# Second block's sparse attention: values padded as the stationary side, weights transposed by reciprocal row sums one feature chunk further on

## The reference, cut to what matters

```python
def sparse_attention(q, k, v, q_idx, k_idx, w_idx, rel_bias):
    ...
        score = jnp.where(s_pos[None, None, :] <= t_pos[None, :, None], score, -jnp.inf)
        _, idx = lax.top_k(score, topk)
    ...
        logits = jnp.where(valid[:, :, None, :], logits, -jnp.inf)
        p = jax.nn.softmax(logits, axis=-1).astype(v.dtype)
        o = jnp.einsum('bqhk,bqkhd->bqhd', p, vs)
        return o.reshape(B, Q_BLOCK, BRANCH_W)
```

## Time and profile before

| | us |
|---|---|
| median of 3 runs | 1947.67 |
| lowest and highest | 1947.66, 1947.9 |
| the profiled execution | 1947.58 |
| its span in the trace | 1945.9 |
| PE busy in it | 1926.0 (99%) |
| DVE busy | 1379.2 (71%) |
| ACT busy | 926.0 (48%) |
| POOL busy | 238.2 (12%) |

### The profile page before, as it was taken

The page is one execution under the profiler, slowest core; times in us unless marked ns, Lnnn a source line. Parts: engine busy times, 40 slices in busy tenths (PEclk is TensorE's granted clock), DMA queues, the critical chain, the costliest instruction groups (busy, mean ns, idle before and its releaser), DMA issues.

```text
span 1945.9 us, 29897 instructions
## 1 busy us (share of the span) xinstructions
PE 1926.0 (99%) x11936; PEld 1721.2 (88%) x11936; DVE 1379.2 (71%) x1577; ACT 926.0 (48%) x1020; POOL 238.2 (12%) x196
## 2 busy tenths in 40 slices
PE   7999999999999999999999999999999999999998
PEld 6999888889998888888899998888888899998887
DVE  7686766677677666766769677667766769677666
ACT  5564433445644443644554445444544554445443
POOL 0000000000001000000049250000000049250000
PEclk9999999999999999999999999999999999999999
DMA  7544555554355555555454455555555454555553
GB/s 269 195 159 152 188 184 192 195 192 173 132 195 205 194 192 175 186 191 181 167 183 152 171 190 191 185 194 175 205 192 181 167 183 152 173 190 180 185 192 108
DMA packets 50483, 353.37 MB, mean 182 GB/s; under 512 B 5921, under 2 KB 6049, under 8 KB 8657
## 3 DMA queue, kind: packets, MB, share of 16 engines
q1 hardware_dynamic: 47952, 341.93, 49.6%
q0 software_dynamic: 2432, 10.04, 1.6%
HBM read 349.85 MB, written 2.10 MB: 181 GB/s over the span
## 4 chain that ended last, share of the span: by engine, by line
PE 89%; DVE 6%; ACT 2%; issue 1%; DMA 0%; DVEq 0%; SPq 0%; POOL 0%; POOLq 0%; ACTq 0%
PE ps L225 19%; PE ps L189 18%; PE ps L191 18%; PE ps L190 18%; PE ps L226 9%; DVE w_lo L165 3%; PE ps L229 3%; PE ps L228 1%; ACT w_hi L158 1%; DVE conv_y L2021 1%; PE ps L1184 1%; DVE score L2069 0%; ACT a L1565 0%; PE ps L2202 0%; DVE top L2064 0%
## 5 line engine op out<-in xcount | busy, mean ns | idle before, releaser
L165 DVE TENSOR_TENSOR w_lo<-raw,w_hi 128x2048 fp32r<-128x2048 f32 x318 | 736.5, 2319 | 283.4 <-ACT w_hi L158 282.3
L158 ACT ACTIVATE w_hi<-raw 128x2048 fp32r<-128x2048 f32 x318 | 608.0, 1916 | 402.3 <-PE ps L191 225.7
L225 PE MATMUL ps<-a,w_hi 128*128 128x512 f32 x1568 | 563.2, 398 | 2.3 <-DVE w_lo L165 1.3
L226 PE MATMUL ps<-a,w_lo 128*128 128x256 f32 x1568 | 439.9, 281 | 0.0
L225 PEld LDWEIGHTS ps<-a,w_hi 128*128 128x128 f32 x1568 | 295.0, 188 | 67.5 <-DVE w_lo L165 2.4
L189 PE MATMUL ps<-mixH,w_hi 128*128 128x256 f32 x1168 | 334.4, 286 | 0.6 <-DVE w_lo L165 0.4
L190 PE MATMUL ps<-mixL,w_hi 128*128 128x256 f32 x1168 | 330.4, 283 | 0.0
L191 PE MATMUL ps<-mixH,w_lo 128*128 128x256 f32 x1168 | 330.3, 283 | 0.0
L189 PE MATMUL ps<-w_hi,mixH 128*128 128x512 f32 x832 | 324.9, 390 | 1.0 <-DVE mixL L397 0.9
L191 PE MATMUL ps<-w_hi,mixL 128*128 128x512 f32 x832 | 323.8, 389 | 0.0
L190 PE MATMUL ps<-w_lo,mixH 128*128 128x512 f32 x832 | 323.7, 389 | 0.0
(11 more groups left out here) (378 smaller groups left out, 2274.8 us busy)
## 6 DMA issues: line engine op xcount, KB each, us to landing
raw<-in_w_b SPq DMA_DIRECT2D x198, 1024.0 KB, 5.0
raw<-in_w_a SPq DMA_DIRECT2D x125, 1024.0 KB, 4.8
rows<-in_post_gains POOLq DMA_DIRECT2D x6, 512.0 KB, 4.1
rows<-in_rows_a POOLq DMA_DIRECT2D x2, 1028.0 KB, 7.1
raw<-in_w_a SPq DMA_DIRECT2D x2, 512.0 KB, 5.9
x<-in_x SPq DMA_DIRECT2D x2, 512.0 KB, 5.9
bias_line<-a_gates POOLq DMA_DIRECT2D x1, 1024.0 KB, 4.2
out<-x SPq DMA_DIRECT2D x4, 256.0 KB, 2.0
```

The source lines that it names most:

```text
L158: act.activation(k.w_hi[:, s, :], k.raw[:, s, :], ACT.Copy).then_inc(k.hi_ready, 1)
L165: dve.tensor_tensor(k.w_lo[:, s, :], k.raw[:, s, :], k.w_hi[:, s, :].bitcast(F32), ALU.subtract).then_inc(k.lo_ready, 1)
L225: pe.matmul(both, hi[:, kt, cols], k.a[:, :, kt, :], start=kt == 0, stop=False)
L226: pe.matmul(high, lo[:, kt, cols], k.a[:, 0, kt, :], start=False, stop=False)
```

## The change

The values `v_tok` are stored padded: each head has 128 columns, of which its own 64 hold values and the other 64 zeros, so that two heads of a pair can be summed into one tile of 128 features. They become the stationary side, the weights `pT` the moving side, and the result comes out by feature in PSUM bank 3, where the transposes of `yb2` put it before; `yb2`, its transposes and VectorE's reciprocals and products go. The division by the row sums moves in front: ScalarE's exponentials write their row sums, GpSimd raises them to the power -1 and multiplies the identity by them (`rdiag`, in the place of `qkF`), and the 12 transposes of the weights become 12 matmuls by these diagonals. These stand behind feature 17 instead of in front of it, the weighted sums stand behind feature 18, and on ScalarE `gate_in(8)` moves in front of the evictions of `pT`. GpSimd's order gets the new work between its last tap and the wait for VectorE's taps.

```diff
-        v_tok = sb("b_v_tok", [P, TT, BH, BD + 1])
+        v_tok = sb("b_v_tok", [P, TT, BH, 2 * BD])
+        v_own = v_tok[:, :, :, :].rearrange("p t (j e) d -> p t j e d", e=2)
+        rdiag = qkF[:, :, :].rearrange("p f n -> p (f n)").rearrange("p (t h n) -> p t h n", t=TT, h=BH)
+        neg_one = sb("neg_one", [P, TT, BH])
...
-        yb2 = sb("yb2", [P, TT, BW])
         gated = [[RL[:, n * 512:(n + 1) * 512] for n in range(3)] + [y0[:, :, :].rearrange("p t n -> p (t n)")],
-                 [GU[:, n * 512:(n + 1) * 512] for n in range(3)] + [yb2[:, :, :].rearrange("p t n -> p (t n)")]]
+                 [GU[:, n * 512:(n + 1) * 512] for n in range(3)] + [idxF[:, :, :].rearrange("p f n -> p (f n)")]]
...
+            pool.memset(neg_one[:, :, :], -1.0).then_inc(zc.sem, zc.one())
+            pool.wait_ge(zc.sem, zc.at(0))
+            pool.memset(v_tok[:, :, :, :], 0.0).then_inc(vzero_ready.sem, 1)
...
                 pool.wait_ge(ch.sem, ch.at(l))
+                pool.wait_ge(exp_ready.sem, exp_ready.at(l, 2))
+                pool.tensor_tensor(rsum[:, :, :], rsum[:, :, :], neg_one[:, :, :], ALU.pow).then_inc(ch.sem, ch.one())
+                pool.wait_ge(ch.sem, ch.at(l))
+                for qt in range(TT):
+                    ins = pool.tensor_tensor(rdiag[:, qt], mid(k.ident, BH), last(rsum[:, qt, :], P), ALU.mult)
+                ins.then_inc(rdiag_ready.sem, 1)
...
+                if l == 0:
+                    act.wait_ge(vzero_ready.sem, vzero_ready.at(0, 1))
                 act.wait_ge(k.chunk_done, st.results(l, M0 + 2))
                 for tt in range(TT):
-                    ins = act.activation(v_tok[:, tt, :, 0:BD], k.ps[:, 0, tt * BW:(tt + 1) * BW].rearrange("p (h n) -> p h n", h=BH),
-                                         ACT.Copy, scale=rho[:, tt:tt + 1])
+                    v = k.ps[:, 0, tt * BW:(tt + 1) * BW].rearrange("p (j e n) -> p j e n", j=2, e=2)
+                    for e in range(2):
+                        ins = act.activation(v_own[:, tt, :, e, e * BD:(e + 1) * BD], v[:, :, e, :], ACT.Copy, scale=rho[:, tt:tt + 1])
                 ins.then_inc(f_evicted.sem, 1)
...
-                                             bias=rmax[:, qt, h:h + 1])
+                                             bias=rmax[:, qt, h:h + 1], accum_out=rsum[:, qt, h:h + 1])
...
                 gate_in(7)
+                gate_in(8)
                 act.wait_ge(pT_done.sem, pT_done.at(l, 1))
...
-                gate_in(8)
...
-            dve.memset(v_tok[:, :, :, BD:BD + 1], 1.0).then_inc(vone_ready.sem, 1)
...
-                dve.wait_ge(pv_done.sem, pv_done.at(l, 1))
-                y2v = yb2[:, :, :].rearrange("p t (j e n) -> p t j e n", j=2, e=2)
-                outs = [k.ps[:, (5, 2)[qt], 0:BH * (BD + 1)].rearrange("p (e j n) -> p e j n", e=2, j=2) for qt in range(TT)]
-                for qt in range(TT):
-                    dve.reciprocal(rsum[:, qt, :].rearrange("p (e j) -> p e j", e=2), outs[qt][:, :, :, BD]).then_inc(ch.sem, ch.one())
-                dve.wait_ge(ch.sem, ch.at(l))
-                for qt in range(TT):
-                    for e in range(2):
-                        ins = dve.tensor_tensor(y2v[:, qt, :, e, :], outs[qt][:, e, :, 0:BD],
-                                                last(rsum[:, qt, 2 * e:2 * e + 2], BD), ALU.mult)
-                ins.then_inc(y2_ready.sem, 1)
...
+                feature(17)
                 pe.wait_ge(exp_ready.sem, exp_ready.at(l, 2))
+                pe.wait_ge(rdiag_ready.sem, rdiag_ready.at(l, 1))
                 for h in range(BH):
                     for kb in range(2):
-                        ins = pe.transpose(k.ps[:, 2 + h // 2, (h % 2) * SEQ + kb * P:(h % 2) * SEQ + (kb + 1) * P], logit[:, h, (1 + kb) * P:(2 + kb) * P], k.ident)
+                        ins = pe.matmul(k.ps[:, 2 + h // 2, (h % 2) * SEQ + kb * P:(h % 2) * SEQ + (kb + 1) * P],
+                                        logit[:, h, (1 + kb) * P:(2 + kb) * P], rdiag[:, 1, h, :], start=True, stop=True)
                 ins.then_inc(pT_done.sem, 1)
                 for h in range(BH):
-                    ins = pe.transpose(k.ps[:, 4, h * P:(h + 1) * P], logit[:, h, 0:P], k.ident)
+                    ins = pe.matmul(k.ps[:, 4, h * P:(h + 1) * P], logit[:, h, 0:P], rdiag[:, 0, h, :], start=True, stop=True)
                 ins.then_inc(pT_done.sem, 1)
-                feature(17)
+                feature(18)
                 pe.wait_ge(pT_ready.sem, pT_ready.at(l, 2))
-                for qt in range(TT):
-                    for h in range(BH):
-                        j, e = head_slot(h)
-                        out = k.ps[:, (5, 2)[qt], (2 * e + j) * (BD + 1):(2 * e + j + 1) * (BD + 1)]
-                        for s in range(qt + 1):
-                            ins = pe.matmul(out, pT[:, 2 * e + j, s + qt, :], v_tok[:, s, h, :], start=s == 0, stop=s == qt)
-                ins.then_inc(pv_done.sem, 1)
-                feature(18)
-                pe.wait_ge(y2_ready.sem, y2_ready.at(l, 1))
-                to_features(3, yb2).then_inc(y2T_done.sem, 1)
+                for j in range(BH // 2):
+                    out = k.ps[:, 3, j * SEQ:(j + 1) * SEQ]
+                    pe.matmul(out, v_tok[:, 0, 2 * j, :], pT[:, j, 0:2, :], start=True, stop=False)
+                    for e in range(2):
+                        pe.matmul(out[:, P:SEQ], v_tok[:, 1, 2 * j + e, :], pT[:, 2 * e + j, 2, :], start=False, stop=False)
+                    ins = pe.matmul(out, v_tok[:, 0, 2 * j + 1, :], pT[:, 2 + j, 0:2, :], start=False, stop=True)
+                ins.then_inc(y2T_done.sem, 1)
```

More of the change, by code:

```diff
@@ L50 @@
 DVE_A = 112
-CARRIED = {n: n for n in ("sc_done", "pT_done", "pT_ready", "pv_done", "max_ready", "exp_ready", "mix_ready", "mixH_ready",
+CARRIED = {n: n for n in ("sc_done", "pT_done", "pT_ready", "max_ready", "exp_ready", "mix_ready", "mixH_ready",
                           "mix_split", "f_evicted")}
@@ L1250 @@
 TAKEN = float(np.float32(-3.3e38))
-DVE_B = 109
-POOL_B = 63
+DVE_B = 107
+POOL_B = 64
 def second_block(nc, k, d, sems, block):
@@ L1365, in second_block @@
         sc_done, l_ready, max_ready, exp_ready = sig("sc_done", 2), sig("l_ready", 2), sig("max_ready", 2), sig("exp_ready", 2)
-        pT_done, pT_ready, pv_done, y2_ready, y2T_done, y2H_ready, y2_split = (
-            sig(n, p) for n, p in (("pT_done", 2), ("pT_ready", 2), ("pv_done", 1), ("y2_ready", 1), ("y2T_done", 1),
+        pT_done, pT_ready, rdiag_ready, y2T_done, y2H_ready, y2_split = (
+            sig(n, p) for n, p in (("pT_done", 2), ("pT_ready", 2), ("rdiag_ready", 1), ("y2T_done", 1),
                                    ("y2H_ready", 1), ("y2_split", 1)))
-        vone_ready = sig("vone_ready", 0)
+        vzero_ready = sig("vzero_ready", 0)
         pmm_done, y1H_ready, y1_split = (sig(n, 1) for n in ("pmm_done", "y1H_ready", "y1_split"))
```

## The result

| | before | after |
|---|---|---|
| median, us (19 runs each) | 1947.62 | 1951.09 |
| lowest to highest | 1947.22 to 1947.93 | 1950.89 to 1952.02 |
| the profiled execution | 1947.58 | 1951.01 |
| its span | 1945.9 | 1949.3 |

The ratio is 1.0018, 95% interval 1.0013 to 1.0024: the changed kernel is 3.47 us slower. The slowdown is clear of noise. At 0.18% it lies just under the 0.2% by which the prediction sorts slower from unchanged, and its interval reaches over that line on the upper side. It is within the stated range of 1950.9 to 1957.3, 0.5 under the forecast of 1951.6.

A forecast was written before the change was run, and what follows sets the result against it. TensorE, busy 99% of the span, was taken to bound the kernel. Layers +1.65 and +2.06 make 3.71, plus 2 x 0.1 gives 3.9: 1951.5 profiled, median 1951.6; range 1950.9 to 1957.3.

The forecast's parts named there:

- Order: On TensorE, chunk 17 directly after chunk 16 still waits for w_lo until 1071.88; 1.6 us idle a layer, transposes move behind.
- The sum from chunk 17 to chunk 20: TensorE, start to start: 23.00 us against 21.35 in layer 0 (+1.65) and 20.94 in layer 1 (+2.06).
- rdiag matmuls: On TensorE behind chunk 17, 12 one-pass transposes become 12 matmuls by a diagonal, 24 passes, 2.60 us.
- padded sums with the chunk behind them: On TensorE behind chunk 18, 8 two-pass matmuls taking 2.53 us, then chunk 19 at 5.83.
- The wait before chunk 20: TensorE's 0.52 us wait for w_lo in layer 0 goes, since all of TensorE is later.
- GpSimd's power: Power of 8 columns after GpSimd's 16 taps: 0.56 plus 7 x 0.14, estimated 1.6 us.
- the power's hold on VectorE: Delay of VectorE while GpSimd's power runs: between 0 and 1.6 us, taken as 0.1 a layer.
- The products: GpSimd's two 512-column products, 1.36 us each, fall on taps after w_lo(17), delaying w_lo(18) by 2.1, covered by 1.0.
- Rival C: GpSimd's power holds the port, so products get ahead of w_lo(17): 2.4 to 3.5 a layer, 1956.2 to 1958.4; chance 0.20.
- Rival B: GpSimd's products slip in first, holding w_lo(17) or making w_lo(18) miss chunk 18: 1.05 a layer, 1953.6; chance 0.15.
- D: Not slower: w_lo(17) arrives during chunk 16, chunk 17 follows at once, 1.6 less a layer, 1948.4; chance 0.05.
- E: The matmuls by the diagonal take one pass like transposes, 1.3 less a layer, 1949.0; chance 0.03.

The follow-up runs named there:

- e1: Changed kernel with VectorE computing w_lo of chunk 17 right behind that of chunk 16, the four taps between them afterwards; 1947.82 us, ratio to before 1.0002.
- e2b: Kernel before with the new order alone, old matmuls, no new GpSimd work, w_lo(21) also ahead of VectorE's wait for the result by feature; 1949.56 us, ratio 1.0011.
- e3: New matmuls in the old order, multiplying by the identity, without GpSimd's power and products; 1947.74 us, ratio to before 1.0002.
- e6: Kernel before with only VectorE's order changed: w_lo(17) right behind w_lo(16), w_lo(20) before the wait for the evicted result; 1946.23 us, ratio 0.9993.
- e5: Changed kernel with GpSimd's power of the row sums replaced by a multiplication of the same tiles; 1957.11 us (1955.33 to 1958.66 in five runs).

## Why the prediction was right, step by step

- *Order*, the deciding step: right. Chunk 17 starts some 1.6 later than an ordinary step and waits for `w_lo`(17), and e1 and e2b show it from both sides: with the wait taken out of the changed kernel, 3.0 to 3.3 come back; with the order put into the kernel before, 2.0 are lost.
- *The sum from chunk 17 to chunk 20*: 23.00 forecast, 23.02 and 23.03 measured. Its terms: rdiag matmuls 2.60 forecast, 2.60 measured (1077.55 to 1080.15); padded sums with the chunk behind them 2.53 + 5.83 = 8.36 forecast, 8.38 measured (1085.98 to 1094.36). Order alone costs 2.0 (e2b), the matmuls alone 0.35 (e3), both 3.5. The traces say why these don't add up. From the end of chunk 16 to chunk 20, e1 (new matmuls) takes 23.02 and e6 (old matmuls) 22.04 in each layer, with hardly a wait in either. So the new matmuls are 1.0 more work a layer, 2.0 in all. The waits beyond that were 0.91 and 0.53 before and are 1.58 and 1.60 in the changed kernel, 1.7 more. The change thus costs about as much by added work as by added waiting: in the old order the old waits pay for most of that work, in the new order nothing does.
- *The wait before chunk 20* is gone, as said.
- *GpSimd's power*: 1.6 forecast from the rise of 0.14 a column, 1.74 measured, and 1.75 in layer 1. The forecast passed over the one row of two columns that took 1.76; why that one was long is open. The 0.1 a layer that I added for the power's hold on VectorE is the mis-sized term: it is 0. Of the 0.5 that the forecast is too high, 0.2 is this term, and the other 0.3 is the part outside the two stretches that isn't explained. The prediction gave slower by over 0.2% the larger chance (0.62, of which rivals B and C were 0.35); the measured 0.18% lies on the other side of that line, though its interval doesn't settle the side.
- *The products*: forecast to hold two taps for 1.05 each; they held two, for some 0.8 each. The cover in front of chunk 18 was 1.6, not 1.0.
- *Rival C*, the power holding the port throughout, doesn't hold here: a tap of 0.47 started behind a power of 1.74 and ran beside it. The SBUF — State Buffer page of the Trainium skill (section "Who interferes with whom") calls the shared port pair an exclusive lock and has a VectorE instruction with two SBUF inputs contend with GpSimd's reads; that whoever issues first has the pair for the whole instruction it says of VectorE's 2-port modes, and the prediction took this over to taps. The power in this trace doesn't agree with the lock; the products agree in kind (1.26 for a tap).
- *Rival B* was a real danger: e5 is that case. What kept it off was that the power is slow. Its price of 1.05 a layer was too low: both products came first and cost 1.62 a layer, and the clock came on top. *D* and *E* are refuted by the 1.70 gap and the 24 records.

## What to carry to other kernels

Before moving work on the engine that bounds the kernel, look at what the work covers where it stands: 12 transposes of 1.2 us that filled part of a wait of 1.6 were free, and 24 passes of 2.6 in the same place lost only what stuck out, 1.0, but behind the wait both cost in full. Where the wait is for another engine that is merely busy with something less urgent, reorder that engine first: moving one `w_lo` in front of four taps was worth nearly as much as the whole change cost. And an operation that is cheaper on its own engine can be dearer for the kernel, if it lets the next one reach a shared resource first.

## What the runs showed of the hardware that was not expected

A stall of TensorE can cost more than its length: after a gap of 3.32 us between matmuls the matmuls ran at 1.2 GHz (granted clock 0.50) for 2.9 us in layer 0, and at 2.4 GHz (1.00) after an equally long one in layer 1 (e5), and the runs of that kernel spread over 3.3 us. The gaps of 1.70 and 1.72 in the changed kernel left the clock at 1.00, as the stretch behind the first of them shows (columns as in e5):

```profile
1071.70:1074.70 3.00, 3.00 (x25) 3.00 (x26) 3.00 (x4) 1.00 (x1) 2.02 (x2) 1.00 0.65 180
```

On GpSimd, how long an operation of two inputs keeps VectorE out doesn't follow how long it lasts: an addition of 512 columns held a tap for 1.05 of its 1.37, a product of 512 columns with broadcast inputs for some 0.8 of its 1.22, a power of 8 columns for nothing of its 1.74. What it does follow, the columns read or the operation, no run here separates.
